# Two attentions of a streaming encoder: unnormalised weights are turned, and the output is scaled by rows and turned back once per head pair

## The reference, cut to what matters

```
def mla_attend(q_lat, q_rope, q_pos, ckv, krope, k_pos):
    s = (... scores ...).astype(jnp.float32) * MLA_SCALE
    visible = (k_pos[None, :] // CHUNK) <= (q_pos[:, None] // CHUNK)
    p = jax.nn.softmax(jnp.where(visible, s, -jnp.inf), axis=-1).astype(ckv.dtype)
    return jnp.einsum('bhqk,bkr->bqhr', p, ckv)

def band_attend(q, k, v, q_pos, k_pos, rel_bias):
    s = jnp.einsum('bqhd,bkhd->bhqk', q, k).astype(jnp.float32) * C_SCALE
    s = s + rel_bias[:, idx].astype(jnp.float32)
    p = jax.nn.softmax(jnp.where(valid, s, -jnp.inf), axis=-1).astype(v.dtype)
    return jnp.einsum('bhqk,bkhd->bqhd', p, v)
```

## Time and profile before

| | |
|---|---|
| median of the runs | 3272.31 us |
| profiled execution, its own time | 3272.54 us |
| its span | 3270.5 us |
| PE busy | 3056.0 us (93%) |
| DVE busy | 1257.3 us (38%) |
| ACT busy | 1015.3 us (31%) |
| POOL busy | 862.5 us (26%) |

### The profile page before, as it was taken

How to read it: one execution, slowest core, us unless ns; L and a number is a source line. 1 busy time by engine, 2 the same in 40 slices (tenths; PEclk the granted TensorE clock), 3 DMA queues, 4 the chain that set the end, 5 groups by cost and what they waited for, 6 DMA issues and landing times. The chain is left out here.

```text
span 3270.5 us, 46685 instructions
## 1 busy us (share of the span) xinstructions
PE 3056.0 (93%) x18884; PEld 2956.9 (90%) x18884; DVE 1257.3 (38%) x2672; ACT 1015.3 (31%) x1772; POOL 862.5 (26%) x437
## 2 busy tenths in 40 slices
PE   6999986888899999999989999999879999999998
PEld 5889976778799999999979899999859999999997
DVE  4423335666622222222243556666653222222223
ACT  4322234444421112121134544444443111121211
POOL 3211122211332223222233322323324222232220
PEclk8999988899999999999999999999999999999999
DMA  3133133111211111111021111111111111112101
GB/s 114 56 73 65 42 143 102 47 44 34 65 52 39 38 38 40 63 38 51 0 69 43 44 37 43 39 41 44 34 48 56 52 38 38 38 38 64 38 13 61
DMA packets 153853, 165.72 MB, mean 51 GB/s; under 512 B 9063, under 2 KB 137015, under 8 KB 153535
## 3 DMA queue, kind: packets, MB, share of 16 engines
q1 hardware_dynamic: 153726, 163.96, 16.4%
HBM read 140.78 MB, written 28.92 MB: 52 GB/s over the span
## 5 line engine op out<-in xcount | busy, mean ns | idle before, releaser
L236 PE MATMUL ffn_banks<-hhi,ffn_whi 128*128 128x384 f32 (+1 forms) x2112 | 693.0, 328 | 19.5 <-POOL hlo L217 13.2
L237 PE MATMUL ffn_banks<-hlo,ffn_whi 128*128 128x384 f32 (+1 forms) x2112 | 692.5, 328 | 0.0
L238 PE MATMUL ffn_banks<-hhi,ffn_wlo 128*128 128x384 f32 (+1 forms) x2112 | 692.3, 328 | 0.0
L1211 DVE TENSOR_TENSOR ffn_act<-ffn_silu,ffn_banks 128x384 f32<-128x384 f32 x132 | 70.2, 532 | 962.3 <-PE ffn_banks L238 945.7
L236 PEld LDWEIGHTS ffn_banks<-hhi,ffn_whi 128*128 128x128 f32 x2112 | 399.5, 189 | 21.0 <-issue 21.0
L1145 POOL TENSOR_TENSOR ffn_wlo<-ffn_stage,ffn_whi 128x2048 fp32r<-128x2048 f32 x66 | 303.3, 4609 | 423.7 <-ACT ffn_whi L1105 423.7
L237 PEld LDWEIGHTS ffn_banks<-hlo,ffn_whi 128*128 128x128 f32 x2112 | 399.3, 189 | 0.0
L238 PEld LDWEIGHTS ffn_banks<-hhi,ffn_wlo 128*128 128x128 f32 x2112 | 399.2, 189 | 0.0
L1217 DVE TENSOR_TENSOR xT<-xT,ffn_banks 128x384 f32<-128x384 f32 (+1 forms) x528 | 281.0, 532 | 240.4 <-PE ffn_banks L238 240.4
L238 PE MATMUL ffn_banks<-ffn_ahi,ffn_wlo 128*128 128x384 f32 (+1 forms) x1056 | 344.7, 326 | 0.0
L237 PE MATMUL ffn_banks<-ffn_alo,ffn_whi 128*128 128x384 f32 (+1 forms) x1056 | 344.6, 326 | 0.0
(11 more groups left out here) (323 smaller groups left out, 5580.9 us busy)
## 6 DMA issues: line engine op xcount, KB each, us to landing
ffn_stage<-in_w_gate SPq DMA_DIRECT2D x22, 1024.0 KB
ffn_stage<-in_w_up SPq DMA_DIRECT2D x22, 1024.0 KB, 5.3
ffn_stage<-in_w_down SPq DMA_DIRECT2D x22, 1024.0 KB, 4.9
mix_wst<-in_w_qkv SPq DMA_DIRECT2D x24, 512.0 KB
mix_wst<-in_w_in SPq DMA_DIRECT2D x22, 512.0 KB
load_xin<-in_x_prompt SPq DMA_DIRECT2D x8, 512.0 KB, 4.6
mix0b_wst<-in_w_out SPq DMA_DIRECT2D x8, 512.0 KB
mix_wst<-in_w_out SPq DMA_DIRECT2D x8, 512.0 KB
```

What stands on the lines that cost most here:

```text
L236: nc.tensor.matmul(out, whi[:, k, :], hhi[:, k, c0:c0 + w], start=(k == 0), stop=False)
L237: nc.tensor.matmul(out, whi[:, k, :], hlo[:, k, c0:c0 + w], start=False, stop=False)
L238: last = nc.tensor.matmul(out, wlo[:, k, :], hhi[:, k, c0:c0 + w], start=False, stop=(k == kts - 1))
L1211: nc.vector.tensor_tensor(act32[:, f, 0:w], silu[:, f, 0:w], banks[:, 2 * f + 1, 0:w], ALU.mult).then_inc(product, 1)
```

## The change

In both attentions:

- `normalise` is gone. DVE keeps the reciprocal of the sums, as `reciprocal(g)` in its own step. `turn(g)` waits for the exponential (`exped`) itself.
- `weigh(g)` has its operands exchanged: the turned exponentials are the stationary operand, 64 columns of V the moving one, and the result in `pO` has queries as rows and 64 columns.
- `evict(g)` on DVE multiplies `pO` by the reciprocals (one per row) into a new SBUF tile `otok`, the even head in columns 0 to 63 and the odd one in 64 to 127. `high` and `low` are gone from the steps, and `weigh(g + 1)` waits for `evicted` in place of `lo`.
- A new filler "flip" is PE's transpose of `otok` for one tile of a pair, after the odd head's `evict`. It is the first filler of the next step (n = 10 to 17, and n = 0 of the next pair), takes one of the three banks `F` in their order, is split by ACT (high part, after `exp(g + 1)`) and DVE (low part, waits for the high part), which empties the bank.
- DVE's order in a step becomes `maximum(g + 1)`, `reciprocal(g)`, all fillers' results (the flip first), `evict(g)`.

In `mix0b_stage` alone SP's loop has the weight load of a step ahead of `load_q` and `load_k`, and `split_w` of ACT waits for one filler in place of three banks.

```diff
@@ mix0b_stage
+    def flips(g):
+        if g == 0:
+            return []
+        pair, n = divmod(g - 1, STEPS)
+        return [("flip", pair, ORDER[1][n - N])] if n >= N else []
+    def work(g):
+        return flips(g) + fillers(g)
...
+                if g in splits:
+                    load_w(splits[g])
                 if i == 2 and h + 2 < B_HEADS:
                     load_q(h + 2)
                 if i == 4 and h + 2 < B_HEADS:
                     load_k(h + 2)
-                if g in splits:
-                    load_w(splits[g])
...
+                if x[0] == "flip":
+                    _, pair, t = x
+                    w = tile_width(t)
+                    pe.wait_ge(s["evicted"], STEPS * pair + N + ORDER[1].index(t) + 1)
+                    if n >= FB:
+                        pe.wait_ge(emptied[n % FB], n // FB)
+                    nc.tensor.transpose(F[:, n % FB, 0:w], otok[0:w, t, :], S["ident"][0:w, 0:w]).then_inc(filled[n % FB], 1)
+                    return
...
-                pe.wait_ge(s["normal"], g + 1)
+                pe.wait_ge(s["exped"], g + 1)
...
-                    pe.wait_ge(s["lo"], g)
+                    pe.wait_ge(s["evicted"], g)
                 for b, (_, kw, vt) in enumerate(tiles):
-                    last = nc.tensor.matmul(pO[:, 0:w], V[0:kw, vt, :], pT[0:kw, b * P:b * P + w],
+                    last = nc.tensor.matmul(pO[0:w, 0:H], pT[0:kw, b * P:b * P + w], V[0:kw, vt, own(e)],
...
-            def high(g):
+            def high(x):
+                _, pair, t = x
+                await_filled(act, x)
+                nc.scalar.activation(out_of(pair, t)[0], F[:, number[x] % FB, 0:tile_width(t)], ACT.Copy).then_inc(s["hi"], 1)
...
                 keep(g)
                 if g + 1 < PAIRS * STEPS:
                     exp(g + 1)
+                for x in flips(g):
+                    high(x)
...
+                if x[0] == "flip":
+                    _, pair, t = x
+                    hi, lo = out_of(pair, t)
+                    dve.wait_ge(s["hi"], flip_no[x] + 1)
+                    v.tensor_tensor(lo, F[:, n % FB, 0:tile_width(t)], hi, ALU.subtract).then_inc(emptied[n % FB], 1)
+                    return
...
+            def evict(g):
+                pair, e, t = step_of(g)
+                w = tile_width(t)
                 dve.wait_ge(s["inverted"], g + 1)
-                v.tensor_scalar(p_[0:w, 0:width], p_[0:w, 0:width], inv[0:w, col], None, ALU.mult).then_inc(s["normal"], 1)
+                dve.wait_ge(s["summed"], g + 1)
+                v.tensor_scalar(otok[0:w, t, own(e)], pO[0:w, 0:H], inv[0:w, g % 4:g % 4 + 1], None, ALU.mult)\
+                 .then_inc(s["evicted"], 1)
...
                 if g + 1 < PAIRS * STEPS:
                     maximum(g + 1)
-                for x in work[:1]:
-                    empty(x)
-                if g + 1 < PAIRS * STEPS:
-                    normalise(g + 1)
-                for x in work[1:]:
+                reciprocal(g)
+                for x in work(g):
                     empty(x)
                 if i == 2 and h + 1 < B_HEADS:
                     split_q(h + 1)
-                low(g)
+                evict(g)
@@ mix1_stage (turn, weigh, evict, high and low parts in the same way)
+        if s > N:
+            x.append(("flip", p, TILES[s - N - 1]))
+        if s == 0 and p:
+            x.append(("flip", p - 1, TILES[-1]))
         if s == 0:
             x += [("vtok", p, 1), ("vtok", p, 2)]
...
-                        pe.wait_ge(s["lo"], STEPS * (pair + 1))
+                        await_emptied(pe, ("flip", pair, TILES[-1]))
```

More of the change, by code:

```diff
@@ L1498, in mix0b_stage @@
     FB = 3
-    number = {x: n for n, x in enumerate(groups)}
+    def flips(g):
[5 more added lines that the diff above has]
+        return flips(g) + fillers(g)
+    END = PAIRS * STEPS
+    program = [x for g in range(END) for x in work(g)] + flips(END) + behind
+    number = {x: n for n, x in enumerate(program)}
+    flip_no = {x: n for n, x in enumerate(x for x in program if x[0] == "flip")}
     def begun(g):
@@ L1546, in step_of, with out_of, await_filled, await_emptied @@
             return pair, e, ORDER[e][i]
-        def out_of(pair, e, t):
+        def out_of(pair, t):
             cols = slice(t * P, t * P + tile_width(t))
-            return [x[own(e), CAT0 + pair, cols] for x in (hhi, hlo)]
+            return [x[:, CAT0 + pair, cols] for x in (hhi, hlo)]
+        def await_filled(eng, x):
+            eng.wait_ge(filled[number[x] % FB], number[x] // FB + 1)
+        def await_emptied(eng, x):
+            eng.wait_ge(emptied[number[x] % FB], number[x] // FB + 1)
         @block.sync
@@ L1700, in _ @@
                     score(g + 1)
-                for x in fillers(g):
+                for x in work(g):
                     fill(x)
                 weigh(g)
-            for x in behind:
+            for x in flips(END) + behind:
                 fill(x)
@@ L1778, in _ @@
                     split_w(splits[g])
-                high(g)
+            for x in flips(END):
+                high(x)
         @block.vector
@@ L1947, in mix1_stage @@
     ahead += [("kc", 0, 0), ("vtok", 0, 0)]
-    behind = [("out", PAIRS - 1, j, c) for j, c in outs]
+    behind = [("flip", PAIRS - 1, TILES[-1])] + [("out", PAIRS - 1, j, c) for j, c in outs]
     def key_of(x):
@@ L2143, in fill @@
                     last = nc.tensor.matmul(dst[:, 0:w], wl, oh, start=False, stop=True)
+                elif kind == "flip":
+                    _, pair, t = x
+                    w = tile_width(t)
+                    pe.wait_ge(s["evicted"], STEPS * pair + N + TILES.index(t) + 1)
+                    last = nc.tensor.transpose(dst[:, 0:w], otok[0:w, t, :], S["ident"][0:w, 0:w])
                 elif kind == "vtok":
@@ L2258, in take @@
                     nc.scalar.activation(kk[own(e), e, T:KEYS], bank(x)[own(e), :], ACT.Copy).then_inc(s["kc_hi"], 1)
+                elif x[0] == "flip":
+                    _, pair, t = x
+                    w = tile_width(t)
+                    await_filled(act, x)
+                    nc.scalar.activation(o_hi[:, pair % 2, t * P:t * P + w], bank(x)[:, 0:w], ACT.Copy).then_inc(s["hi"], 1)
                 elif x[0] == "ktok":
@@ L2287, in keep @@
                         .then_inc(s["p_kept"], 1)
-            def high(g):
-                pair, e, t = step_of(g)
-                w = tile_width(t)
-                act.wait_ge(s["summed"], g + 1)
-                nc.scalar.activation(o_hi[own(e), pair % 2, t * P:t * P + w], pO[own(e), 0:w], ACT.Copy).then_inc(s["hi"], 1)
             norm.square(act, 0)
@@ L2333, in _ @@
                     split_w(unit_no[weights_at(pair, n)])
-                high(g)
+            take(behind[0])
         @block.vector
```

79 lines of the change are left out of this document (34 added, 45 removed).

## The result

The changed kernel takes 3238.5 us (median of 4 runs, 3236.6 to 3239.7), the kernel before 3273.5 (4 runs): ratio 0.989, 95% interval 0.987 to 0.990, so 35 us less. The forecast was 15 us less. The profiled execution took 3239.7 us, its span is 3238.0.

A forecast was written before the change was run, and what follows sets the result against it. The prediction took PE as the bound, busy in nine tenths of the span; its terms, -54 - 11 + 2 + 13 + 16 + 34 - 12 - 3, gave -15 us on 3272.5, so 3257 us, range 3226 to 3277.

The forecast's parts named there:

- scaling off the chain: Both attention loops: the turn needs only exp, so PE's waits for the scaled tile go; -54 us, bounds -40 to -60.
- SP's order: Latent steps 11 and 31: weight load issued ahead of load_q and load_k ends late weights; -12 us together.
- weighing and its sample steps: Both attentions: 64 moving columns save 0.05 us in 216 steps, -11 us; sample steps' second tile-shape switch, +2 us.
- what the flip holds: PE waits for the flip's bank until exp, high and low parts are done: +16 us latent, +34 us band.
- flips, and all that is left: Forecast for flips: 108 one-pass transposes on PE at 0.12 us each with the hand-over, +13 us.
- ends: First turns, a query split held up by POOL and the clock after it, -4; last output groups, +1: -3 us.
- 24 of 28: Band attention's share of the scaling gain: 24 us of PE's 12.6 + 15.4 us of waits for the scaled tile.
- a second switch of tile shape, 24 by 0.1: Sample steps of the weighing: each of 24 pays 0.1 us for another change of tile shape, +2 us.
- 1 (the bank hardly holds PE): Rival: the flip's 16 + 34 us of bank waits are mostly not paid; 3224 us, chance 0.12.
- 2 (the clock falls): Rival: PE idling in four steps of each of six band pairs lowers the clock; 3293 us, chance 0.12.
- 3 (weights still late): Rival: another wait ahead in SP's queue still delays the weight load; +12, 3269 us, chance 0.08.
- 4 (narrow weighing is cheap): Rival: 1776 weighing passes each save 0.055 us, 98 us of PE work; 3190 us, chance 0.03.

The follow-up runs named there:

- e1: Kernel before with only SP's order changed in the latent attention, weight load ahead of query and key loads: 3262.3 us, ratio 0.997.
- e2: Kernel before without the scaling of the exponentials in both attentions, outputs left unscaled: 3205.8 us, ratio 0.979.
- e9: Kernel before with the scaling cut to the first 64 columns in every step, the rest left unscaled: 3239.8 us, ratio 0.991.
- e7: Changed kernel with SP's order undone, weight load again behind the query and key loads: 3254.4 us, ratio 0.995.
- e5: Changed kernel with all 128 columns of V weighed in both attentions, the eviction reading its own head's 64: 3247.4 us, ratio 0.993.
- e4: Changed kernel with ACT taking the flip's high part ahead of exp(g + 1) instead of behind it: 3196.2 us, ratio 0.976.
- e6: The kernel of e4 with every flip's transpose issued twice into the same bank: 3198.8 us, ratio 0.978.
- e8: The kernel of e4 with the latent attention's weight loads issued three steps earlier in SP's program: 3192.1 us, ratio 0.976.
- e3: Changed kernel with each flip as last filler of its step instead of first, in both attentions: 3218.5 us, ratio 0.983.
- e10: The kernel of e8 with the band attention's flips as last filler at n = 10, 15, 16 and 0: 3193.7 us, ratio 0.977.

## Why the prediction was right or wrong

The direction was right, and so was each mechanism but one, the price of the sample tile's weighing. The sum was 19 to 20 us too timid. By terms, each with the run that isolates it (e1, e2 and e9 on the kernel before, the others on the changed one, so the row by subtraction also holds what the parts do to each other):

| term | forecast | loops | from |
|---|---|---|---|
| scaling off the chain | -54 | -62 | e2 |
| SP's order | -12 | -13 | changed against e7 (-10.7 by e1) |
| weighing and its sample steps | -11 + 2 | -16 | changed against e5 |
| what the flip holds | +16 + 34 | +43 | changed against e4 |
| flips, and all that is left | +13 | +14 | by subtraction |
| ends | -3 | - | the loops' part in the rows above |
| sum | -15 | -34 | measured: -30.8 and -3.0 in the loops |

**The scaling** was mis-sized by 8, or by some 5 without what the forecast booked under its ends. The step that failed is the bound by wait rows: "24 of 28" (the "30 of the 31.9" held: -31.9). Wait rows for the scaled tile don't hold the copies queued behind the scaling (3.5 us), nor the weight loads that start late after a short stall. Where the chain is the longest part it was read rightly: in the last band pair steps of 4.02 us became 3.23.

**The weighing** was mis-sized by 7. That a pass keeps 0.11 us at 64 moving columns held (1.22 us for ten against 1.27), and so did the 0.05 per step. The step that failed is the sample tile: "a second switch of tile shape, 24 by 0.1" was taken from ten passes with 128 weight columns, while the swap makes the sample tile the weights, with 64 columns. No row of before had that form, and I gave it no bound below nothing. It was about -0.5 us a step in the band attention (e5), and not +0.1. The Trainium skill says in "TensorE: Matmul & The Clock Gate", "LDWEIGHTS (loading the stationary operand)", that a weight load takes its columns divided by 1.2 ns, so 107 ns for 128 and 53 for 64. The rows agree for three forms (112 ns for 128 weight columns, whatever moves; 58 for 64 with 64 moving), and that rule, applied to the swapped operands, would have pointed to this gain. It isn't the whole price: with 64 weight columns and 128 moving, e5 shows 109.

**The hold** was mis-sized by 7, again toward the gain: it cost less. In the band loop it was +24 for +34. Against e4, n = 15 and 16 have 1.16 each for 1.6, n = 17 has 0.4 for "gives 1.0", n = 0 has 0.5 for 1.35, n = 11 has 0.3 for 0.2 and n = 13, not forecast, 0.2: 3.7 a pair for 5.7. The steps that failed most are n = 17 and n = 0. At n = 17 the next exp has 128 columns and takes 0.40 us, and I had carried over too much of the wide steps' tail. At n = 0 the step did rise by 1.2, but 0.7 of it comes with the flip's place as first filler and stands in the row of the flips. e4 still holds the bank for 0.9 us, so these are lower bounds: against the kernel before, n = 15 and 16 rose by 1.44. In the latent loop the hold cost 19 for 16, of which 13.9 in its own steps and the rest in steps at a lower clock, two of them ahead of any flip (e4); step 11 rose by 1.6 as forecast:

```profile
568.11 1.06 ACT L1741 ACTIVATE mix0b_whi<-mix0b_wst 128x1024 fp32r<-128x1024 f32 x1
568.25 0.29 DVE L1824 TENSOR_TENSOR hlo<-mix0b_F,hhi 128x128 fp32r<-128x128 f32 x1 [1.16 <-ACT hhi L1780]
...
568.60 0.44 PE L1665 MATMUL mix0b_F<-hhi,mix0b_whi 128*128 128x384 f32 x1 [1.35 <-DVE hlo L1824]
```

The first row is also the mark for SP's order: ACT starts on the weights in step 11 with no wait, against 8.44 us in the earlier trace rows.

**The flips** held in sum, by subtraction only, and that is partly luck: e6 puts the pure PE work at 7 us where 13 were forecast, so the other 7 of the 14 are places and leftovers that no run separates.

**The ends** can't be told from the other rows. What they name did happen inside the loops: the two first steps lost 0.9 and 1.4 us and step 21 of the latent attention 3.2, some 2 more than its neighbours of the same kind, together 4.2 for 4. Behind the last latent turn the output groups start 1.7 us later (2.6 before, 4.3 now) for 1. The first turn lies 3 us earlier, but in e1 as well.

**The rivals.** 1 (the bank hardly holds PE): refuted, e4 gets 43 us back by it. 2 (the clock falls): refuted, PE's clock is 0.99 over the band loop. 3 (weights still late): refuted for steps 12 and 32, by the row above and e1. But step 22 still waits 3.5 us for `pT` behind unit 3's weights, which the forecast passed over ("In the other four weight steps the order doesn't matter"); an earlier load gives 6.5 us there (e8). 4 (narrow weighing is cheap): refuted for 192 steps, true for the 24 sample steps. The size came from none of them: three terms missed by 7 to 8 us each, all three toward the gain.

## What to carry to other kernels

When an instruction leaves a queue, count not only the waits that name it but the waits for what stood behind it, and look for short stalls in the weight loads' idle time as well as the matmuls'. When a difference of a few us is read from loops, first look which steps ran at a lower clock, and whether the edit acts there at all. When one new step shares a bank with the fillers, first look where its reader stands in the other engine's order: moving one activation ahead of exp was worth more (42 us) than the whole change (35). When operands are swapped, look for each tile form that the swap creates; if no row of before shows one, bound it to both sides.

## What the runs showed of the hardware that was not expected

- Weighing passes with 64 weight columns and 64 moving columns start 58 ns apart, with 128 of either 109 to 112 ns: neither operand alone sets the pace.
- A DVE tensor_scalar from SBUF to SBUF of 128x256 f32 took 0.35 us without a neighbour. Beside a subtraction of GpSimd it took between 0.51 and 2.55 us and each time (159 cases in the 13 traces) ended 0.15 to 0.16 us after GpSimd did: it waited for the rest of that instruction. The Trainium skill, "SBUF — State Buffer", "SBUF: two separate sides", names the shared port as an exclusive lock; these rows agree. The change took the scalings out of it: the evictions that replace them read PSUM and took at most 0.29 us in all 58 cases beside GpSimd, as without it. The set-up of the near bias still waits for GpSimd, and n = 17 was 1.4 to 2.9 us longer by that in e3 and 1.8 in e10 (3.5 once, at a lower clock).
- A transpose of one 128x128 tile repeated into the same bank cost 0.06 us on average, and nothing in steps that wait for a bank.
- The granted clock fell to 0.62 to 0.71 in single latent steps (12, 30, 54) of the changed kernel. The same steps ran at full clock in other kernels, and steps 1 and 2 had 0.50 and 0.79 or the full clock with no edit near them.
